# A hybrid mLSTM / GLA / S5 encoder on one core: GpSimd's masks and first exponents earlier, weight splits between the scans, a table stored tile by tile

## The chip, the core and the metric

The kernel runs on one core of one Trainium2 chip. The metric is the device time of one execution in microseconds (us). The core has five engines that run their own instruction streams and meet at semaphores: TensorE (PE in the rows; its weight loads are PEld), VectorE (DVE), ScalarE (ACT), GpSimd (POOL) and SyncE (SP, which here only issues DMAs). ACTq and SPq are the instruction queues of ACT and SP, where DMAs are issued.

## The reference

The input is 256 positions of 2048 channels in float32, through two layers.

- Layer 0: an RMS norm, one combined projection (`w_in`), which feeds an mLSTM (8 heads) and a gated linear attention, GLA (4 heads of 128 key channels), then an output projection (`w_out`), and a residual.
- Layer 1: an RMS norm, an S5 layer (a diagonal complex state space of 64 states for each of 128 groups of channels), GELU and a gate (`glu`), and a residual.
- Behind each: an RMS norm and a convolutional FFN (`up`, a causal convolution of width 3, SiLU times value, `down`, with 5504 inner channels). A last RMS norm ends it.

What the change touches, cut from the reference:

```python
mqk = silu(causal_dwconv(concat([mq, mk]), m_conv_w, m_conv_b))     # width 4
lf = log_sigmoid(f_pre); b = cumsum(lf)                             # mLSTM: sums and a running maximum
log_a = log_sigmoid(glr @ g_w_gate + g_b_gate) / G_TAU              # GLA's forget gate
Bc = cumsum(log_a)
A = einsum("bhtd,bhsd,bhtsd->bhts", qc, kc, exp(Bc_t - Bc_s))       # only for s <= t
lam_bar = exp(lam * dt); pow_t = exp(lam * dt * steps)              # S5: powers of complex numbers
```

## The kernel before, in words

Everything is kept transposed, channels on the 128 partitions and the 256 positions along the row. Each product is done in float32 to more than the precision of one fp32r product. A **block** of weights (128x1024, 512 KB) is loaded by SP into `raw`; ACT writes its rounded part to `hi` (`act_split`, L298), DVE the rest to `lo` (`dve_split`, L305), and PE multiplies both with the two parts `xh`, `xl` of the activations (`pe_tile`). The three rings have four slots; SP refills a slot of `raw` when DVE has split it (`lo_done`), ACT refills one of `hi` when PE has used it (`block_used`). One output tile of 128 channels takes two blocks and goes to one of two banks of PSUM, `acc[q % 2]`. ACT copies one half of the bank (`low_half`), DVE adds the other (`joined`) and counts the tile as read (`tile_read`).

The order on each engine is that of the code in its block function; nothing reorders it. Each waits on semaphores in that order. The stages in order of time:

1. The first norm (to about 27 us). POOL makes constants, then waits for DVE's step sizes of S5 (`s5_dt_new`).
2. Tiles of the gates, of the GLA's q and k (8 tiles) and of the mLSTM's q and k (8 tiles, with a convolution of width 4 on DVE: `conv_tile`, and a SiLU: `silu`). Between the two sets stand DVE's scans: the GLA's running sums `decay` (four, L1184), which `lf_new` announces to POOL, and the mLSTM's rows (L1187 to L1191), announced by `rows_new`. DVE splits two blocks ahead of the tile that it then reads.
3. The values, 32 blocks in 8 steps of 4 (`value_blocks`, L1618 to L1620), and between them the GLA's levels. For level m POOL writes differences of `decay` to `xk` (L667 and L668, `gla_x`), ACT takes the exponential (L857), DVE multiplies by q and k (`gla_scale`, L1243 and L1244), and PE multiplies (`gla_level`, L1641 and L1647). In each step DVE does two splits, then `gla_scale`, then two more splits. From level 1 on, DVE reads a mask made by POOL (`masks_ready`).
4. The output gates with the mLSTM's heads, `w_out`, and the FFN of layer 0. While `w_out` runs, POOL builds the table of S5's turns (`rot_c`, `rot_s`, each 128 x 64 x 64). It lies where the later tiles of the FFN's activations will be written, so it has to be in DRAM (`s5_rot`) before tile `ROT_FREE` = 19 of `up`.
5. `down`, S5, `glu` and the second FFN.

POOL's own stream in stages 2 and 3, before: 8 halvings of an exponential by complex products (L591 to L611), S5's powers (L617 to L635), the seven masks (L637 to L644), the sum of `ident`'s blocks (L650), `skip` (L653), and only then the differences for the GLA.

The loop over `up` is `up_pair(i)`, two tiles a pass: ACT does two splits, `high`, `low_half`, two splits, a tanh and `low_half`; DVE two splits, the product, a convolution, two splits, `low` and a convolution.

Of the kernel before, what the change touches and what calls it, by code (L numbers as in the profile page):

```python
# [13 lines left out]
P = 128  # L14
D = 2048
L = 256
KT = D // P
# [3 lines left out]
M_HEADS, M_DV, M_DK = 8, 128, 64  # L21
# [4 lines left out]
S5_P, S5_N = 16, 64  # L26
# [12 lines left out]
ROT_FREE = 19  # L39
# [56 lines left out]
def hybrid_encoder(nc, t, out):  # L96
# [6 lines left out]
    with ctx:  # L103
# [456 lines left out]
        def _(g):  # L560
# [8 lines left out]
            for j in range(T5):  # L569
                G.memset(steps[:, j, :, :, j], 1.0)  # L570

# [37 lines left out]
            for _ in range(HALVINGS):  # L609
                G.tensor_scalar(zv(14), cur[0], 2.0, None, ADD)  # L610
                chain(G.tensor_scalar(zv(15), cur[1], 1.0, None, MUL))  # L611
                cmul(nxt, cur, (zv(14), zv(15)), ztmp)
                cur, nxt = nxt, cur
            ztmp = (z(12), z(13))
# [22 lines left out]
            chain(G.memset(masks[:, :, :], 0.0))  # L637
            n = P // 2
            for m in range(7):
                v = masks[:, m, :].rearrange("p (j w) -> p j w", w=2 * n)  # L640
                chain(G.memset(v[:, :, n:], 1.0))
                chain(G.affine_select(out=v, in_=v, compare_op=ALU.is_ge, fill=0.0, base=0,
                                      pattern=[[-2 * n, P // (2 * n)], [0, 2 * n]], channel_multiplier=1))
                ins = G.affine_select(out=v, in_=v, compare_op=ALU.is_ge, fill=0.0, base=n - 1,  # L644
                                      pattern=[[2 * n, P // (2 * n)], [0, 2 * n]], channel_multiplier=-1)
                chain(ins) if m < 6 else ins.then_inc(masks_ready, 1)
                n //= 2
            chain(G.memset(rtmp[:, 0, 0:S5_P], 0.0))
            for x in range(P // S5_P):
                chain(G.tensor_tensor(rtmp[:, 0, 0:S5_P], rtmp[:, 0, 0:S5_P],  # L650
                                      ident[:, S5_P * x:S5_P * (x + 1)], ADD))
# [6 lines left out]
            g.wait_ge(lf_new, 1)  # L658
            n = P
            for m in range(8):  # L660
                s = m % 2
                if m >= 2:
                    g.wait_ge(gla_mm, m - 1)
                v = xk[:, s, :, :].rearrange("p h (j a w) -> p (h j) a w", a=2, w=n)
                b = decay[:, :, :].rearrange("p h (j a w) -> p (h j) a w", a=2, w=n)
                mid = b[:, :, 0, n - 1:n].broadcast_to([P, G_HEADS * L // (2 * n), n])
                G.tensor_tensor(v[:, :, 0, :], mid, b[:, :, 0, :], SUB)  # L667
                G.tensor_tensor(v[:, :, 1, :], b[:, :, 1, :], mid, SUB).then_inc(gla_x, 1)  # L668
                n //= 2
# [135 lines left out]
        def _(a):  # L805
# [120 lines left out]
            def ffn(b_up, b_dn, q_up, n, layer):  # L926
# [18 lines left out]
                if layer == 0:  # L945
                    with a.Fori(1, 4) as i:
                        up_pair(i, False)
                    a.wait_ge(rot_whole, 1)
# [166 lines left out]
        def _(v):  # L1115
# [63 lines left out]
            V.memset(neg_m, 0.0)  # L1179
            v.wait_ge(ln_done, 1)  # L1180
            V.scalar_tensor_tensor(rows[:, 3, :], rows[:, 1, :], 0.0, rows[:, 2, :], MIN, SUB)
            chain(V.scalar_tensor_tensor(xk[:, 0, :, :], xk[:, 1, :, :], 0.0, xk[:, 0, :, :], MIN, SUB))
            for x in range(G_HEADS):
                ins = V.tensor_tensor_scan(decay[:, x, :], ones_l[:, :], xk[:, 0, x, :], 0.0, MUL, ADD)  # L1184
            ins.then_inc(lf_new, 1)

            chain(V.tensor_tensor_scan(rows[:, 2, :], ones_l[0:M_HEADS, :], rows[:, 3, :], 0.0, MUL, ADD))  # L1187
            chain(V.tensor_tensor(rows[:, 3, :], rows[:, 0, :], rows[:, 2, :], SUB))
            chain(V.tensor_tensor_scan(rows[:, 5, :], rows[:, 3, :], rows[:, 3, :], 0.0, MAX, MAX))
            V.tensor_scalar(neg_m[0:M_HEADS], rows[:, 5, :], -1.0, None, MUL)  # L1190
            V.tensor_tensor(rows[:, 4, :], rows[:, 2, :], rows[:, 5, :], ADD).then_inc(rows_new, 1)  # L1191

# [21 lines left out]
            def conv_tile(i, m):  # L1214
                dve_split(v, B_IN + 20, 4, i, range(2 * m, 2 * m + 2))
# [5 lines left out]
            conv_tile(0, 0)  # L1221
            conv_tile(0, 1)
# [796 lines left out]
```

## Time and profile before

| | |
|---|---|
| median of 3 runs | 2178.53 us (2175.89 to 2179.95) |
| the profiled execution's own time | 2178.51 us |
| its span in the trace | 2176.8 us |
| PE busy | 2062.1 us, 95% |
| DVE busy | 1600.1 us, 74% |
| ACT busy | 983.6 us, 45% |
| POOL busy | 600.0 us, 28% |
| mean granted clock of TensorE | 0.977 |
| DMA | 398.78 MB, mean 183 GB/s |

The busy share is a mean over the whole span. An engine that is busy 95% of the time still has stretches in which it waits, and a wait in the timeline is shown in brackets behind the instruction that ended it, with what released it. A POOL that is idle for most of the span can still be the last to finish what another engine needs.

### The profile page before, as it was taken

The page shows a single profiled execution, that of the slowest core. Times are in us where ns is not written, and L with a number is a line of the kernel's source. Part 1 is how long each engine was busy: PE and PEld are TensorE (multiplying, and loading weights), DVE is VectorE, ACT ScalarE, POOL GpSimd, SP SyncE. Part 2 cuts the span into 40 slices and gives each one's busy share as a digit, 9 for nine tenths or more (in the row PEclk, how much of TensorE's full clock was granted, in tenths as well). Part 3 has the DMA queues.
Part 4 walks back from the last instruction along what each step waited for, and adds up shares of the span by engine and source line. Part 5 has one row for each costly group of instructions (what it writes and reads, how often), then busy time and mean ns, then how long its engine had stood idle before and what let it go on. Part 6 is the DMA issues. An engine that isn't in the chain of part 4 may idle for free.

```text
span 2176.8 us, 39816 instructions
## 1 busy us (share of the span) xinstructions
PE 2062.1 (95%) x13014; PEld 1790.2 (82%) x13014; DVE 1600.1 (74%) x2333; ACT 983.6 (45%) x1391; POOL 600.0 (28%) x686
## 2 busy tenths in 40 slices
PE   5979999998999999999999977989999999999997
PEld 4757877887888888888888876878888888888886
DVE  7766554777788888888777675778888888875655
ACT  5434344444444444444555513454444444444442
POOL 6991100590000000007888564510000000001221
PEclk9999999998999999999999988999999999999999
DMA  4535533453755555556778884545555555556664
GB/s 167 172 116 168 160 129 124 142 186 121 247 191 193 191 185 185 190 190 197 236 231 235 252 258 135 191 139 186 187 192 192 187 187 187 191 183 195 188 182 140
DMA packets 146680, 398.78 MB, mean 183 GB/s; under 512 B 22704, under 2 KB 47920, under 8 KB 146624
## 3 DMA queue, kind: packets, MB, share of 16 engines
q1 hardware_dynamic: 126176, 379.17, 55.3%
q10 hardware_dynamic: 20448, 18.88, 2.7%
q8 instruction: 33, 0.54, 0.1%
q14 instruction: 23, 0.19, 0.0%
HBM read 377.02 MB, written 18.87 MB: 182 GB/s over the span
## 4 chain that ended last, share of the span: by engine, by line
PE 44%; DVE 26%; issue 14%; POOL 7%; DVEq 3%; ACT 2%; DMA 2%; ACTq 1%; SPq 0%; POOLq 0%
PE bank L325 21%; PE bank L324 11%; DVE lo L305 9%; DVE cgv L1201 4%; DVE cgv L1198 3%; DVE sumt L339 3%; DVE th L1394 2%; ACT lowt L334 1%; DVE aa L1398 1%; DVE cgv L1393 1%; PE bank L1618 1%; PE bank L1620 1%; PE bank L1619 1%; DVEq L1201 1%; PE bank L321 1%
## 5 line engine op out<-in xcount | busy, mean ns | idle before, releaser
L325 PE MATMUL bank<-xx,hi 128*128 128x512 f32 x3420 | 1199.7, 393 | 0.0
L305 DVE TENSOR_TENSOR lo<-raw,hi 128x1024 fp32r<-128x1024 f32 x698 | 881.4, 1294 | 106.4 <-ACT hi L298 104.9
L324 PE MATMUL bank<-xx,lo 128*128 128x256 f32 x3420 | 957.4, 280 | 0.0
L298 ACT ACTIVATE hi<-raw 128x1024 fp32r<-128x1024 f32 x698 | 710.5, 1053 | 324.6 <-PE bank L325 254.9
L325 PEld LDWEIGHTS bank<-xx,hi 128*128 128x128 f32 x3420 | 642.3, 188 | 133.2
L324 PEld LDWEIGHTS bank<-xx,lo 128*128 128x128 f32 x3420 | 644.7, 189 | 10.9 <-issue 0.4
L325 PE MATMUL bank<-aa,hi 128*128 128x512 f32 x1344 | 467.7, 392 | 0.0
L324 PE MATMUL bank<-aa,lo 128*128 128x256 f32 x1344 | 376.1, 280 | 4.7 <-DVE lo L305 4.7
L325 PEld LDWEIGHTS bank<-aa,hi 128*128 128x128 f32 x1344 | 252.4, 188 | 54.4
L324 PEld LDWEIGHTS bank<-aa,lo 128*128 128x128 f32 x1344 | 252.4, 188 | 7.4 <-DVE lo L305 6.0
L1201 DVE SCALAR_TENSOR_TENSOR cgv<-sumt,par,cgv 128x255 f32<-128x255 f32 x368 | 179.5, 488 | 54.4 <-DVE cgv L1201 26.1
L339 DVE TENSOR_TENSOR sumt<-bank,lowt 128x256 f32<-128x256 f32 x212 | 89.5, 422 | 128.6 <-ACT lowt L334 128.0
L933 ACT ACTIVATE aa<-th 128x256 f32 (+1 forms) x86 | 35.9, 418 | 322.8 <-DVE th L1394 322.8
L334 ACT ACTIVATE lowt<-bank 128x256 f32<-128x256 f32 x212 | 80.0, 377 | 214.2 <-PE bank L325 206.4
L345 POOL TENSOR_TENSOR ssq<-h 128x256 f32<-128x256 f32 x2 | 3.0, 1490 | 531.8 <-DVE h L1373 509.8
L733 POOL MEMSET k_win<- 128x256 f32 x1 | 0.3, 314 | 493.9 <-PE bank L325 493.9
L321 PE MATMUL bank<-xx,hi 128*128 128x512 f32 x228 | 93.2, 409 | 15.7 <-DVE lo L305 15.7
L1198 DVE TENSOR_SCALAR cgv<-sumt,par 128x256 f32<-128x256 f32 x180 | 74.8, 416 | 40.7 <-DVE sumt L339 40.4
L1372 DVE TENSOR_TENSOR h<-bank,h 128x256 f32 (+1 forms) x48 | 20.4, 424 | 104.6 <-PE bank L325 103.0
L348 POOL TENSOR_TENSOR sqt<-h 128x256 f32<-128x256 f32 x28 | 40.4, 1443 | 201.2 <-DVE h L1373 166.0
L1618 PE MATMUL bank<-hi,xx 128*128 128x512 f32 x128 | 53.1, 415 | 15.7 <-DVE lo L305 15.7
L759 POOL TENSOR_TENSOR sumt<-bbar,pow_in 128x256 f32<-128x256 f32 x64 | 63.6, 1013 | 2.5
(333 smaller groups left out, 1968.2 us busy)
## 6 DMA issues: line engine op xcount, KB each, us to landing
raw<-in_up SPq DMA_DIRECT2D x344, 512.0 KB, 3.8
raw<-in_down SPq DMA_DIRECT2D x160, 448.0 KB, 4.1
raw<-in_w_in SPq DMA_DIRECT2D x98, 512.0 KB, 4.0
raw<-in_w_out SPq DMA_DIRECT2D x32, 512.0 KB, 3.4
raw<-in_down SPq DMA_DIRECT2D x32, 512.0 KB, 3.6
raw<-in_glu SPq DMA_DIRECT2D x32, 512.0 KB, 3.8
s_c<-cp ACTq DMA_DIRECT2D x16, 256.0 KB, 5.0
s_p<-ut ACTq DMA_DIRECT2D x32, 128.0 KB, 5.2
```

The lines of the kernel that those rows point to most:

```text
L298: A.activation(hi[:, s, :], raw[:, s, :], ACT.Copy).then_inc(hi_done, 1)
L305: V.tensor_tensor(lo[:, s, :], raw[:, s, :], hi[:, s, :].bitcast(f32), SUB).then_inc(lo_done, 1)
L321: TE.matmul(bank[:, :], hi[:, s, w], x2[:, k, :, :], start=True, stop=False)
L324: TE.matmul(bank[:, L:], lo[:, s, w], x2[:, k, 0, :], start=False, stop=False)
L325: last = TE.matmul(bank[:, :], hi[:, s, w], x2[:, k, :, :], start=False, stop=k == total - 1)
L334: A.activation(lowt[:, q % 2, :], acc[q % 2][:, L:], ACT.Copy, **kw).then_inc(low_done, 1)
L339: return V.tensor_tensor(sumt[:, q % 2, :], acc[q % 2][:, 0:L], lowt[:, q % 2, :], ADD)
L759: ins = G.tensor_tensor(pq_pt[:, d], bbar[:, s, :, d, :].unsqueeze(3).broadcast_to([P, 4, S5_P, T5]), pow_in[:, pairs, :, (part + d) % 2]. ...
L1198: chain(V.tensor_scalar(o[:, :], x, par[:, bass.ds(base + taps - 1, 1)], par[:, bass.ds(base + taps, 1)], MUL, ADD))
L1201: ins = V.scalar_tensor_tensor(o[:, d:L], x[:, 0:L - d], par[:, bass.ds(base + taps - 1 - d, 1)], o[:, d:L], MUL, ADD)
L1394: V.scalar_tensor_tensor(th[:, 1, :], cg[:, :], 0.5, cv[:, :], MUL, MUL).then_inc(a_new, 1)
L1618: TE.matmul(banks[half][:, :], xh[:, k, r], hi[:, s, w], start=k == 0, stop=False)
```

## The change

Four edits.

- **POOL.** The masks and the sum of `ident`'s blocks go to the front of POOL's stream, ahead of its wait for the step sizes. The differences for the GLA become a function, `gla_exponents(m)`. Those of levels 0 and 1 are done behind the halvings and ahead of S5's powers; the others stay where they were.
- **DVE.** The splits of the blocks for the first two convolution tiles (`B_IN + 20` and its three successors) were two ahead of each `conv_tile`, both behind all scans. Now two stand ahead of the scans of `decay`, one behind these, and one behind the first `conv_tile`. The rows of the mLSTM go behind that.
- **PE.** In a loop `pe_tile` also waits for `tile_read` where it had none (the tiles with q = 1 plus a multiple of two).
- **ACT.** The table of turns was stored with two DMAs of 2048 KB behind the fourth pass of `up`. Now each of 16 passes issues two DMAs of 128 KB, those of one tile.

```diff
-            if q >= 2:
+            if q >= 2 or not isinstance(q_i, int):
                 p.wait_ge(tile_read, q - 1 + q_i)
...
                 cmul(nxt, cur, (zv(14), zv(15)), ztmp)
                 cur, nxt = nxt, cur
+            def gla_exponents(m):
+
+                s, n = m % 2, P >> m
+                if m >= 2:
+                    g.wait_ge(gla_mm, m - 1)
...
+            g.wait_ge(lf_new, 1)
+            gla_exponents(0)
+            gla_exponents(1)
...
-            g.wait_ge(lf_new, 1)
-            n = P
-            for m in range(8):
...
+            for m in range(2, 8):
+                gla_exponents(m)
...
                 if layer == 0:
-                    with a.Fori(1, 4) as i:
-                        up_pair(i, False)
                     a.wait_ge(rot_whole, 1)
-                    for part, x in enumerate((rot_c, rot_s)):
-                        a.dma_start(s5_rot[:, :, part, :].rearrange("k p n -> p k n"),
-                                    x[:, :, :].rearrange("p (k m) c -> p k (m c)", m=4)).then_inc(rot_out, 16)
-                    with a.Fori(4, ROT_FREE) as i:
+                    with a.Fori(1, KT + 1) as i:
                         up_pair(i, False)
-                    a.wait_ge(rot_out, 32)
+                        for part, x in enumerate((rot_c, rot_s)):
+                            a.dma_start(s5_rot[bass.ds(i - 1, 1), :, part, :].squeeze(0),
+                                        x[:, bass.ds(4 * i - 4, 4), :].rearrange("p m c -> p (m c)")
+                                        ).then_inc(rot_out, 16)
+                    with a.Fori(KT + 1, ROT_FREE) as i:
+                        up_pair(i, False)
+                    a.wait_ge(rot_out, 32 * KT)
```

On DVE, around the scans between the GLA's tiles and the mLSTM's (`decay` is written by the four scans, `sumt` by `joined`, `cgv` by the convolution, `mqk` by `silu`), the kernel before has:

```order
L1179 MEMSET sqt 12x256
L1181 SCALAR_TENSOR_TENSOR ut<-ut 8x256
L1182 SCALAR_TENSOR_TENSOR xk<-xk 128x1024
L1184 SCALAR_TENSOR_TENSOR decay<-ones,xk 128x256 x4
L1187 SCALAR_TENSOR_TENSOR ut<-ones,ut 8x256
L1188 TENSOR_TENSOR ut<-ut 8x256
L1189 SCALAR_TENSOR_TENSOR ut<-ut 8x256
L1190 TENSOR_SCALAR sqt<-ut 8x256
L1191 TENSOR_TENSOR ut<-ut 8x256
L305 TENSOR_TENSOR lo<-raw,hi 128x1024 x2
L339 TENSOR_TENSOR sumt<-bank,lowt 128x256
```

and the changed kernel, in the same place:

```order
L305 TENSOR_TENSOR lo<-raw,hi 128x1024 x2
L1215 MEMSET sqt 12x256
L1217 SCALAR_TENSOR_TENSOR ut<-ut 8x256
L1218 SCALAR_TENSOR_TENSOR xk<-xk 128x1024
L1220 SCALAR_TENSOR_TENSOR decay<-ones,xk 128x256 x4
L305 TENSOR_TENSOR lo<-raw,hi 128x1024
L339 TENSOR_TENSOR sumt<-bank,lowt 128x256
L1190 TENSOR_SCALAR cgv<-sumt,par 128x256
L1193 SCALAR_TENSOR_TENSOR cgv<-sumt,par,cgv 128x255
L1193 SCALAR_TENSOR_TENSOR cgv<-sumt,par,cgv 128x254
L1193 SCALAR_TENSOR_TENSOR cgv<-sumt,par,cgv 128x253
L305 TENSOR_TENSOR lo<-raw,hi 128x1024
```

Two splits have gone ahead of the scans, and one each to both sides of the first convolution; the five rows on `ut` and `sqt` follow the last row shown.

On POOL, at the end of the halvings and of S5's powers (`powers` and `r_step` belong to S5, `xk` and `decay` to the GLA), before:

```order
L634 TENSOR_TENSOR r_step<-nt 128x64
L635 TENSOR_SCALAR powers<-powers 128x320
L637 MEMSET masks 128x896
L641 MEMSET masks 128x64
L642 AFFINE_SELECT masks<-masks 128x128
```

and now, at the end of the halvings:

```order
L611 TENSOR_TENSOR nt<-nt 128x128
L612 TENSOR_TENSOR nt<-nt 128x128
L637 TENSOR_TENSOR xk<-decay 128x4x128
L638 TENSOR_TENSOR xk<-decay 128x4x128
L637 TENSOR_TENSOR xk<-decay 128x8x64
L638 TENSOR_TENSOR xk<-decay 128x8x64
L647 MEMSET powers 128x64
```

The four writes of `xk` stand ahead of `powers`, where before `powers` and the masks stood ahead of them.

## Rows read from the trace of the kernel before

**Rows 1.** The timeline of PE, where it waited (start us, duration us; [wait, releaser]).

```profile
91.89 0.80 PE L321 MATMUL bank<-xx,hi 128*128 128x512 f32 x1 [4.67 <-DVE lo L305]
...
145.59 0.50 PE L1618 MATMUL bank<-hi,xx 128*128 128x512 f32 x1 [2.98 <-DVE lo L305]
...
165.44 0.80 PE L1618 MATMUL bank<-hi,xx 128*128 128x512 f32 x1 [12.42 <-DVE lo L305]
179.00 1.05 PE L1641 MATMUL bank<-xk 128*128 128x128 f32 x8
```

**Rows 2.** The timelines of DVE and ACT where the values begin.

```profile
162.21 1.44 DVE L1243 TENSOR_TENSOR xk<-xk,gqk 128x512 f32<-128x512 f32 x1 [15.04 <-ACT xk L857]
...
161.12 1.06 ACT L857 ACTIVATE xk<-xk 128x1024 f32<-128x1024 f32 x1 [16.65 <-POOL xk L668]
```

**Rows 3.** The timeline of POOL from the halvings' end to the first differences.

```profile
118.84 0.64 POOL L597 TENSOR_TENSOR nt<-nt 128x128 f32<-128x128 f32 x1
...
146.80 0.84 POOL L637 MEMSET masks<- 128x896 f32 x1
...
154.33 0.71 POOL L642 TENSOR_SCALAR_AFFINE_SELECT masks<-masks 128x128 f32<-128x128 f32 x1
...
159.04 1.04 POOL L667 TENSOR_TENSOR xk<-decay 128x512 f32<-128x512 f32 x1
...
162.04 1.06 POOL L668 TENSOR_TENSOR xk<-decay 128x512 f32<-128x512 f32 x1
```

**Rows 4.** Windows: length, busy time (instructions) by engine, PE's granted clock, DMA.

```profile
165.40:170.40 5.00, 4.96 (x12) 3.89 (x13) 4.60 (x5) 1.51 (x2) 0.00 (x0) 0.50 0.70 213
```

**Rows 5.** The timeline of DVE around the scans.

```profile
84.69 3.25 DVE L1184 TENSOR_TENSOR_SCAN decay<-ones,xk 128x256 f32<-128x256 f32 x4
...
90.63 2.34 DVE L305 TENSOR_TENSOR lo<-raw,hi 128x1024 fp32r<-128x1024 f32 x2
...
99.80 0.42 DVE L339 TENSOR_TENSOR sumt<-bank,lowt 128x256 f32<-128x256 f32 x1 [0.92 <-ACT lowt L334]
```

**Rows 6.** Timelines where the table is stored: ACT's queue, DVE, PE.

```profile
549.81 4.79 ACTq L950 DMA_DIRECT2D s_rot<-rot_s  x1
...
555.96 2.36 DVE L305 TENSOR_TENSOR lo<-raw,hi 128x1024 fp32r<-128x1024 f32 x2 [4.08 <-ACT hi L298]
...
557.24 0.51 PE L321 MATMUL bank<-xx,hi 128*128 128x512 f32 x1 [2.55 <-DVE lo L305]
...
563.54 0.50 PE L321 MATMUL bank<-xx,hi 128*128 128x512 f32 x1 [0.48 <-DVE lo L305]
```

**Rows 7.** An earlier pass of `up`, at the same place: ACT and DVE.

```profile
538.02 0.39 ACT L334 ACTIVATE lowt<-bank 128x256 f32<-128x256 f32 x1 [1.63 <-PE bank L325]
538.42 2.01 ACT L298 ACTIVATE hi<-raw 128x1024 fp32r<-128x1024 f32 x2
...
540.67 2.36 DVE L305 TENSOR_TENSOR lo<-raw,hi 128x1024 fp32r<-128x1024 f32 x2
```

**Rows 8.** DMAs issued by ACT in `down`: one line (durations ns), then the timeline.

```profile
L1024 ACTq DMA_DIRECT2D s_p<-ut x32: 622/626/741, 1019.4 to 1253.9; - x32
...
1037.58 2.01 ACT L298 ACTIVATE hi<-raw 128x1024 fp32r<-128x1024 f32 x2 [2.22 <-issue]
```

**Rows 9.** The first norm: timelines of PE, ACT, POOL; a window (DVE is third).

```profile
13.51 0.98 PE L1569 MATMUL bank<-ones,ssq 128*128 128x1 f32 x4 [13.51 <-DVE ssq L1136]
...
16.17 0.26 ACT L370 ACTIVATE root_t<-bank,par 128x2 f32<-128x2 f32 x1
...
19.30 0.15 POOL L575 MEMSET nt<- 128x64 f32 x1 [16.32 <-DVE nt L1146]
...
8.30:13.40 5.10, 0.00 (x0) 0.00 (x0) 4.79 (x5) 2.99 (x3) 0.00 (x0) 1.00 1.02 401
```

**Rows 10.** POOL and DVE at the same time, with the inputs of both in SBUF.

```profile
36.37 2.69 POOL L593 TENSOR_TENSOR nt<-nt 128x128 f32<-128x128 f32 x1
...
36.39 2.34 DVE L305 TENSOR_TENSOR lo<-raw,hi 128x1024 fp32r<-128x1024 f32 x2
```

More of the change, by code:

```diff
@@ L570, in _ @@
                 G.memset(steps[:, j, :, :, j], 1.0)
+            chain(G.memset(masks[:, :, :], 0.0))
+            n = P // 2
+            for m in range(7):
+                v = masks[:, m, :].rearrange("p (j w) -> p j w", w=2 * n)
+                chain(G.memset(v[:, :, n:], 1.0))
+                chain(G.affine_select(out=v, in_=v, compare_op=ALU.is_ge, fill=0.0, base=0,
+                                      pattern=[[-2 * n, P // (2 * n)], [0, 2 * n]], channel_multiplier=1))
+                ins = G.affine_select(out=v, in_=v, compare_op=ALU.is_ge, fill=0.0, base=n - 1,
+                                      pattern=[[2 * n, P // (2 * n)], [0, 2 * n]], channel_multiplier=-1)
+                chain(ins) if m < 6 else ins.then_inc(masks_ready, 1)
+                n //= 2
+            chain(G.memset(rtmp[:, 0, 0:S5_P], 0.0))
+            for x in range(P // S5_P):
+                chain(G.tensor_tensor(rtmp[:, 0, 0:S5_P], rtmp[:, 0, 0:S5_P],
+                                      ident[:, S5_P * x:S5_P * (x + 1)], ADD))
             TWO_PI = (6.28125, 1.9350051879882812e-3, 3.0199157663e-7)
@@ L613, in _ @@
                 cur, nxt = nxt, cur
+            def gla_exponents(m):
+                s, n = m % 2, P >> m
+                if m >= 2:
+                    g.wait_ge(gla_mm, m - 1)
+                v = xk[:, s, :, :].rearrange("p h (j a w) -> p (h j) a w", a=2, w=n)
+                b = decay[:, :, :].rearrange("p h (j a w) -> p (h j) a w", a=2, w=n)
+                mid = b[:, :, 0, n - 1:n].broadcast_to([P, G_HEADS * L // (2 * n), n])
+                G.tensor_tensor(v[:, :, 0, :], mid, b[:, :, 0, :], SUB)
+                G.tensor_tensor(v[:, :, 1, :], b[:, :, 1, :], mid, SUB).then_inc(gla_x, 1)
+            g.wait_ge(lf_new, 1)
+            gla_exponents(0)
+            gla_exponents(1)
             ztmp = (z(12), z(13))
@@ L635, in _ @@
             chain(G.tensor_scalar(powers[:, :, :, 2], powers[:, :, :, 1], -1.0, None, MUL))
[L637 to L651, printed above, removed]
             g.wait_ge(params_in, 16)
@@ L1177, in _ @@
                     gqk_tile(i, m)
[L1179 to L1191, printed above, removed]
             def conv(q, low, used, o, base, taps):
@@ L1212, in silu, with conv_tile @@
                                              cgv[:, 0:1, :], ADD, MUL))
-            def conv_tile(i, m):
-                dve_split(v, B_IN + 20, 4, i, range(2 * m, 2 * m + 2))
+            def conv_tile(i, m, split=True):
+                if split:
+                    dve_split(v, B_IN + 20, 4, i, range(2 * m, 2 * m + 2))
                 if m == 1:
@@ L1220, in conv_tile @@
                 conv(9 + m, 9 + m + 2 * i, 10 + m + 2 * i, cg, COLS["mconv"] + 5 * (2 * i + m), 4)
-            conv_tile(0, 0)
-            conv_tile(0, 1)
+            dve_split(v, B_IN + 20, 4, 0, range(2))
+            V.memset(neg_m, 0.0)
+            v.wait_ge(ln_done, 1)
+            V.scalar_tensor_tensor(rows[:, 3, :], rows[:, 1, :], 0.0, rows[:, 2, :], MIN, SUB)
+            chain(V.scalar_tensor_tensor(xk[:, 0, :, :], xk[:, 1, :, :], 0.0, xk[:, 0, :, :], MIN, SUB))
+            for x in range(G_HEADS):
+                ins = V.tensor_tensor_scan(decay[:, x, :], ones_l[:, :], xk[:, 0, x, :], 0.0, MUL, ADD)
+            ins.then_inc(lf_new, 1)
+            dve_split(v, B_IN + 20, 4, 0, range(2, 3))
+            conv_tile(0, 0, False)
+            dve_split(v, B_IN + 20, 4, 0, range(3, 4))
+            chain(V.tensor_tensor_scan(rows[:, 2, :], ones_l[0:M_HEADS, :], rows[:, 3, :], 0.0, MUL, ADD))
+            chain(V.tensor_tensor(rows[:, 3, :], rows[:, 0, :], rows[:, 2, :], SUB))
+            chain(V.tensor_tensor_scan(rows[:, 5, :], rows[:, 3, :], rows[:, 3, :], 0.0, MAX, MAX))
+            V.tensor_scalar(neg_m[0:M_HEADS], rows[:, 5, :], -1.0, None, MUL)
+            V.tensor_tensor(rows[:, 4, :], rows[:, 2, :], rows[:, 5, :], ADD).then_inc(rows_new, 1)
+            conv_tile(0, 1, False)
             with chain.loop(1, 4, 2 * 4) as i:
```

11 lines of the change are left out of this document (1 added, 10 removed).

## The prediction, as it went on record

> **What bounds the kernel now.** I read the page first: PE is busy 95% of the span, so the time is PE's work plus the few stretches in which it stands still, and a change that leaves PE's work alone can gain only from these. The view of who waited for whom, limited to PE, then names them, and the timelines of PE, ACT, DVE and POOL around each show what ended it.
>
> The longest is at 165.44 us, where PE has stood for 12.42 us for a split of DVE [rows 1]. Follow it back. DVE's split stood behind its first product for the GLA, at 162.21, for which it had waited 15.04 us [rows 2]. That waited for ACT's exponential at 161.12, and ACT had waited 16.65 us for POOL's differences [rows 2]. POOL was not waiting at all: it ended the halvings at 119.48, was in S5's powers until 146.8, in the masks, the sum of `ident`'s blocks and `skip` until 159.04, and then wrote the differences of levels 0 and 1, until 163.10 [rows 3]. Nothing of what it did between is needed by the first level. So the wait is one of order on POOL. Behind it PE also ran at the lower of its two levels: 5.00 us at a granted clock of 0.50, that is at 1.2 in place of 2.4 GHz [rows 4].
>
> The second place is `up`, where ACT's queue spent 4.79 us on issuing the second half of the table. DVE lost 4.08 us on it and PE 2.55 us, and 0.48 us a tile later [rows 6]. The third is at 91.89, where PE stood 4.67 us because all scans stood ahead of the splits [rows 1, 5]. That one must not be counted as a gain without more: see below.
>
> **The POOL edit.** The masks and the sum took at most 146.80 to 159.04, 12.2 us [rows 3]. At the front they run from about 3.0 us (POOL had stood still for 16.32 us before 19.30) to about 15.2 us, ahead of the wait for the step sizes, which ended at 19.30 [rows 9]. They cost POOL nothing. The halvings then end at 119.5 as before. The differences of levels 0 and 1 took 159.04 to 163.10, 4.1 us [rows 3], and now run from 119.5 to 123.6. S5's powers end at 146.8 + 4.1 = 150.9. The next differences wait for PE's first level, which will come later than that, so POOL is not late again.
>
> Next I ask what is late in its place. ACT was free for the exponential at 161.12 - 16.65 = 144.47, DVE for the product at 162.21 - 15.04 = 147.17 [rows 2]. The exponential takes 1.06 us, so it ends at 145.5, ahead of DVE. From DVE's product to PE's first matmul on the block behind it were 165.44 - 162.21 = 3.23 us [rows 1, 2], so this block is ready at 147.17 + 3.23 = 150.4. PE had used up its older blocks at 165.44 - 12.42 = 153.02. PE is later by 2.6 us, so its wait goes whole: **12.42 us**. Nothing takes its place; the 2.98 us before 145.59 [rows 1] are DVE's split behind the convolutions, which the edit leaves. The low clock goes with the long standstill: 5.00 us at half speed did the work of 2.5, a gain of **2.5 us**. The clock's fall at 145.59, behind the shorter wait, stays.
>
> **The DVE edit.** From the scans to the values DVE is the bound: PE waits for a split of DVE at nearly each tile there, and DVE's timeline has hardly a gap. The edit takes no work from DVE. What it can gain is DVE's own idle time: 0.92 us at 99.80 [rows 5], where DVE waited for a tile that PE had started late, at 91.89. Now PE gets its two blocks ahead of the scans and starts this tile at 91.89 - 4.67 = 87.2. PE's wait of 4.67 us does not vanish, though, it moves. A tile takes PE about 5.8 us (557.24 to 563.54 less the wait of 0.48 [rows 6]), so two tiles on, at 98.8, it wants two blocks more. DVE has the same work as before up to the read at 99.80, so it comes to this at 98.9; a convolution and a split later, at about 103, it has the block. PE will stand there for about 4 us. That costs nothing as long as DVE is the bound, since DVE reads the tile that PE then starts only behind two pairs of splits (2.34 us a pair [rows 5]) and another convolution, some 8 us later. Against the 0.92 us stands that the four differences of POOL now fall beside DVE's work, at 119.5 to 123.6. The bounds are a gain of 0.9 us, if they hold DVE up not at all, and a loss of 4.1 - 0.9 = 3.2 us, if DVE stands for their whole length. POOL was busy beside DVE there before, too, so I take a gain of **0.7 us**, near the first bound.
>
> PE's new wait for `tile_read` bites at one place only, the tile that starts at about 93 us: it needs the first convolution's tile to be read. DVE does that behind the scans, the two splits ahead of them and one more: 84.69 + 3.25 + 2.34 + 1.17 = 91.5 us, and PE comes at 87.2 + 5.8 = 93. It costs nothing that shows.
>
> **The first norm.** The masks now run beside DVE's sums of squares. PE's first matmul waits for these, and ends at 13.51 + 0.98 = 14.49, but ACT's root comes at 16.17 [rows 9], behind ACT's own work. So the sums have 1.7 us in hand. From 8.3 to 13.4 us DVE does five sums in 4.79 us [rows 9], each of two inputs in SBUF. At 36.37 an instruction of POOL lasted 2.69 us, to the end of the two splits of DVE that ran from 36.39 [rows 10]: each of the two engines can hold the other. The longest instruction of the masks took 0.71 us [rows 3]. If each of the five sums stood behind one such, they would end 3.6 us later, of which 1.9 us show; if none did, nothing. I take zero, since the sum of the masks' selects is small in this stretch.
>
> The Trainium skill's page "SBUF — State Buffer", section "Who interferes with whom", says that a VectorE instruction with two SBUF inputs and a GpSimd instruction that reads SBUF exclude each other for their whole length, and that whichever issues second blocks. The row at 36.37 agrees. By that rule the upper end of 1.9 us could come about, and it is kept as a rival.
>
> **The ACT edit.** The 4.79 us of issuing go, and with them the 2.55 + 0.48 = **3.03 us** of PE. In their place 16 passes issue two DMAs of 128 KB each. DMAs of 128 KB issued by ACT took 0.62 to 0.74 us each, and three DMAs with their registers held ACT for 2.22 us [rows 8]. So two hold it for 1.3 to 1.7 us. What do they delay? ACT's two splits, which came right behind `low_half`, at 538.42; the first ended at 539.4, and DVE wanted it at 540.67 [rows 7]: 1.2 us in hand. Behind that DVE is ahead of PE by 4.08 - 3.03 = 1.05 us [rows 6], so PE sees nothing until ACT is late by 2.3 us a pass. The issue also begins while `low_half` still runs. So it is hidden, at a price of 0; bounds are 0 and, should two DMAs hold ACT as long as twice the 2.22 us, 16 x (4.44 - 2.3) = 34 us. The value is near the first bound, because two DMAs are less than the three that took 2.22. The table has landed long before the wait at pass 19, two passes of two tiles behind the last store.
>
> **The sum.** 12.42 + 2.5 + 0.7 + 3.03 = 18.65 us. The profiled execution took 2178.51 us (its span 2176.8, and 1.7 around it), and the median of the runs is 2178.53, so no correction is needed: 2178.5 - 18.6 = **2159.9 us**. Behind each of the places all engines wait for each other in the same order as before, and no transfer or chain runs on its own clock over a stage, so a shift is carried to the end.
>
> **Rivals.**
> - *The stores cost passes of `up`.* For it: they are on ACT, whose splits DVE needs, and DVE and PE keep pace almost exactly there. Against it: the 2.3 us in hand. If two DMAs hold ACT for 2.6 us, each pass loses 0.3 us, 16 x 0.3 = 5 us: 2165. Chance 0.10.
> - *Slower than before.* The same mechanism, in its strong form: the queue holds the issuing engine whenever earlier descriptors have not drained, as the second DMA's 4.79 us may be read. At 0.5 + 4.79 = 5.3 us a pass, PE would lose 16 x (5.3 - 2.3) = 48 us: 2208. It decides from 2.3 + 18.6 / 16 = 3.5 us a pass. Against it: the 4.79 us came behind 2 MB, not 128 KB, and three DMAs of `down` took 2.22. Chance 0.03.
> - *The lock in the first norm* costs its 1.9 us: 2162. Chance 0.07.
> - *POOL holds DVE in the convolutions*: the differences and the powers, which now also run beside DVE's first products, cost 3 us: 2163.5. Chance 0.08.
> - *The wait for the first level is not gone but only taken over*, by something between POOL and ACT that I do not see, and half of 14.9 us is lost: 2167. Chance 0.03.
> - *More than forecast*: PE's short standstill at 145.59 and its low clock shrink, too, because DVE comes out of the convolutions earlier than by 0.7: 2156. Chance 0.07.
>
> **How the numbers follow.** The forecast has 0.62, with 2158 to 2162 as its own range. Two tenths outside: 2157 at the low end takes in all but the last rival, and 2165.5 at the high end takes in the norm, POOL and the usual form of the stores. Slower by over 0.2% (4.4 us, about what a measurement of this kernel can tell from no change) is the second rival, 0.03; within it 0.01; faster 0.96.
>
> **What would show it.** Right: ACT's first exponential at about 144 us with no wait for POOL; no wait of PE between 150 and 164; the first level (before at 179.00) at about 163.4; a granted clock of 1.00 from 153 on; a wait of PE of 4 to 5 us at about 103 and none at 92; no wait of PE in `up` behind the table; S5's powers ending at about 151. Wrong: a wait of PE at each of the first 16 passes of `up` (the stores); ACT's root later than 16.2 us (the norm); DVE's first product for the GLA later than 147.2 (DVE held by POOL); a wait for POOL's differences of level 2.

## The result and the profile after

| | before | after |
|---|---|---|
| median | 2177.35 us (2175.89 to 2179.95, 4 runs) | 2162.21 us (2160.33 to 2163.56, 4 runs) |
| ratio, with its 95% interval | | 0.9929 (0.9911 to 0.9946) |
| the profiled execution's own time, span | 2178.51, 2176.8 us | 2161.42, 2159.7 us |
| mean granted clock | 0.977 | 0.980 |

The change gains 15.1 us by the medians; 18.65 had been forecast against a before of 2178.5. The time, 2162.2, lies 2.3 us above the forecast of 2159.9, inside the range and 0.2 us outside the likeliest case's own.

The timeline of PE after, where it waited up to the values, and the first level:

```profile
97.54 0.39 PE L324 MATMUL bank<-xx,lo 128*128 128x256 f32 x1 [0.45 <-DVE lo L305]
104.95 0.80 PE L321 MATMUL bank<-xx,hi 128*128 128x512 f32 x1 [4.36 <-DVE lo L305]
126.47 0.50 PE L321 MATMUL bank<-xx,hi 128*128 128x512 f32 x1 [2.21 <-DVE lo L305]
...
166.15 1.05 PE L1651 MATMUL bank<-xk 128*128 128x128 f32 x8
```

The 12.42 us at 165.44 [rows 1] are gone and nothing took their place. The wait of 4.67 us at 91.89 [rows 1] has become one of 4.36 at 104.95: moved, not removed. The 2.21 us at 126.47 stand behind the convolution that runs beside POOL's four differences (before, the wait at this tile was 0.72 us). The first level is at 166.15 in place of 179.00; about 163.4 had been forecast. The window that held the low clock [rows 4] lay at 165.4 us; over 145 to 170 us the rows of both kernels are (PE is the second number, PE's granted clock stands behind POOL's):

```profile
145.00:170.00 25.00, 11.99 (x35) 9.17 (x36) 9.95 (x11) 5.79 (x6) 15.86 (x37) 0.67 0.25 79
```

```profile
145.00:170.00 25.00, 22.73 (x95) 18.09 (x95) 17.00 (x17) 12.09 (x13) 15.19 (x16) 0.93 0.52 168
```

The first is before, the second after: PE is busy for 22.7 us in place of 12.0, at a clock of 0.93 in place of 0.67. ACT and DVE after, at the first exponential and product, which answer to [rows 2]:

```profile
146.47 1.04 ACT L862 ACTIVATE xk<-xk 128x1024 f32<-128x1024 f32 x1
...
148.92 0.69 DVE L1253 TENSOR_TENSOR xk<-xk,gqk 128x512 f32<-128x512 f32 x1
```

Neither has a bracket: the waits of 16.65 and 15.04 us are gone. Both come later than foreseen, by 2.0 and 1.7 us. POOL after, against [rows 3]:

```profile
120.49 1.04 POOL L637 TENSOR_TENSOR xk<-decay 128x512 f32<-128x512 f32 x1
...
123.73 1.24 POOL L638 TENSOR_TENSOR xk<-decay 128x512 f32<-128x512 f32 x1
...
155.03 1.34 POOL L665 TENSOR_SCALAR powers<-powers 128x320 f32<-128x320 f32 x1
...
167.35 1.04 POOL L637 TENSOR_TENSOR xk<-decay 128x512 f32<-128x512 f32 x1 [9.34 <-PE bank L1651]
```

The differences are written 38 us earlier. S5's powers end at 156.4, not at 151, and then POOL waits for PE 9.34 us, so it is never the last at level 2.

The table's store after, against [rows 6] (ACT's queue, then ACT):

```profile
515.95 0.42 ACTq L955 DMA_DIRECT2D s_rot<-rot_c  x1
516.57 0.36 ACTq L955 DMA_DIRECT2D s_rot<-rot_s  x1
517.36 2.01 ACT L298 ACTIVATE hi<-raw 128x1024 fp32r<-128x1024 f32 x2 [1.23 <-issue]
```

Each of the 16 passes holds ACT for 1.1 to 1.2 us, and PE has no wait above 0.2 us between 505 and 570 us.

**Where the time went, along the program.** PE runs the same 13014 matmuls in the same order in all kernels of this study, so the start of the same matmul can be compared. The table gives its shift against before (median over six neighbours; minus is earlier), each in one profiled execution.

| matmul that starts, before, at | 30 | 140 | 180 | 250 | 528 | 575 | 1200 | end |
|---|---|---|---|---|---|---|---|---|
| after | +1.3 | +2.9 | -12.9 | -12.9 | -11.1 | -14.7 | -15.2 | -17.1 |
| masks back behind the powers | +0.1 | +0.8 | -15.6 | -15.6 | -13.7 | -17.3 | -17.7 | -25.0 |
| without DVE's and PE's edit | +1.5 | +3.5 | -12.1 | -12.1 | -10.2 | -13.8 | -14.3 | -11.3 |
| before + differences ahead | -0.2 | +1.8 | -15.3 | -15.4 | -12.9 | -12.2 | -12.7 | -15.3 |
| before + masks at the front | +1.5 | +2.0 | -10.1 | -10.1 | -10.0 | -10.1 | -9.8 | -13.8 |
| before + table by tiles | -0.2 | +0.1 | +0.5 | +0.5 | +2.2 | -1.3 | -1.8 | -5.7 |
| before + DVE's and PE's edit | +0.1 | -1.0 | +0.8 | +0.8 | +2.5 | +3.4 | +2.9 | -2.2 |
| powers late | -0.2 | +1.5 | -16.2 | -16.2 | -16.2 | -19.7 | -20.2 | -22.1 |
| five halvings late | -0.4 | -3.3 | -19.1 | -19.1 | -19.7 | -23.2 | -23.7 | -23.9 |
| the same kernel again | -0.2 | -2.3 | -18.5 | -18.5 | -18.9 | -22.5 | -23.0 | -30.4 |
| six halvings late, masks earlier | -0.1 | -2.8 | -18.9 | -18.9 | -19.3 | -22.8 | -23.3 | -27.4 |

Read after from left to right: 1.3 us lost in the first norm, 1.6 more in the convolutions, 15.8 gained at the values, 1.8 lost again by 528 us (most of it in the first tiles of the FFN), 3.6 gained at the table, 0.5 in `down`, and 1.9 in S5, where the change does nothing. The last column needs care: two executions of one kernel (rows nine and ten of the table) stand 0.7 us apart at 1200 and 6.5 apart at the end. The windows from 1200 to 1500 us of the two (columns as above):

```profile
1200.00:1500.00 300.00, 261.65 (x2700) 231.83 (x2699) 217.08 (x337) 121.90 (x191) 109.88 (x90) 0.93 0.62 191
```

```profile
1200.00:1500.00 300.00, 266.57 (x2741) 236.11 (x2740) 222.94 (x347) 124.95 (x195) 110.52 (x91) 0.94 0.64 197
```

The second was granted a clock of 0.94 where the first had 0.93, and got further in the same 300 us. A clock higher by 0.01 over 300 us makes, as an estimate, 3 us; the rest of what they differ by is not traced here. So up to 1200 us the traces are compared below, and the end is left to the medians. The same two rows also say how far two executions of one kernel differ ahead of that: 1.0 us at 140, 0.6 at 180 and 0.7 at 1200. A difference between two kernels that is no larger is not shown by one trace of each.

### The profile page after: what moved, and what is told of

It is laid out like the page before. It is cut to its first block, busy times and chain, and to the rows that moved or that the text cites. A ratio compares the mean times of both kernels' runs of the same rounds, so it can differ in the third digit from the quotient of the medians.

```text
span 2159.7 us, 39918 instructions
## 1 busy us (share of the span) xinstructions
PE 2057.3 (95%) x13014; PEld 1787.2 (83%) x13014; DVE 1602.3 (74%) x2333; ACT 983.2 (46%) x1391; POOL 609.9 (28%) x686
## 4 chain that ended last, share of the span: by engine, by line
PE 46%; DVE 30%; issue 14%; DVEq 3%; ACT 2%; POOL 1%; DMA 1%; ACTq 1%; POOLq 0%
PE bank L325 22%; PE bank L324 11%; DVE lo L305 11%; DVE cgv L1193 5%; DVE cgv L1190 3%; DVE sumt L339 3%; DVE th L1404 2%; ACT lowt L334 1%; DVE cgv L1403 1%; PE bank L1628 1%; PE bank L1630 1%; PE bank L1629 1%; DVE aa L1408 1%; PE bank L321 1%; DVEq L1193 1%
## 5 line engine op out<-in xcount | busy, mean ns | idle before, releaser
L324 PE MATMUL bank<-xx,lo 128*128 128x256 f32 x3420 | 959.2, 280 | 0.4 <-DVE lo L305 0.4
L1193 DVE SCALAR_TENSOR_TENSOR cgv<-sumt,par,cgv 128x255 f32<-128x255 f32 x368 | 180.6, 491 | 54.4 <-DVE cgv L1193 26.1
L322 PE MATMUL bank<-xx,lo 128*128 128x256 f32 x228 | 64.3, 282 | 0.0
```

Source lines behind the costliest of these rows:

```text
L322: last = TE.matmul(bank[:, L:], lo[:, s, w], x2[:, k, 0, :], start=False, stop=False)
L324: TE.matmul(bank[:, L:], lo[:, s, w], x2[:, k, 0, :], start=False, stop=False)
L1193: ins = V.scalar_tensor_tensor(o[:, d:L], x[:, 0:L - d], par[:, bass.ds(base + taps - 1 - d, 1)], o[:, d:L], MUL, ADD)
```

## The experiments

**Masks back.** From the changed kernel, masks and sum go back behind the powers; all else stays.

```diff
-            chain(G.memset(masks[:, :, :], 0.0))
...
             chain(G.tensor_scalar(powers[:, :, :, 2], powers[:, :, :, 1], -1.0, None, MUL))
+            chain(G.memset(masks[:, :, :], 0.0))
...
             for m in range(2, 8):
                 gla_exponents(m)
```

> The changed kernel with the masks and the sum of ident's blocks back behind S5's powers. Theory (the masks at the front hold up DVE's sums of squares): ACT's root at 16.2 us in place of 17.6, 1.4 us less: 2160.8 us. POOL then ends the masks at about 167 us, and the differences of level 2 come 1 to 3 us later than in the changed kernel, which DVE's splits behind them have in hand. Rival (the first norm is late for another reason): root at 17.6 us and 2162.2 us.

Measured: 2159.48 us (2148.92 to 2161.77, 6 runs), ratio to before 0.9909 (0.9887 to 0.9930). The interval reaches that of the changed kernel, so the times alone don't decide between them. The trace does. ACT's root is where it was before [rows 9]:

```profile
16.14 0.26 ACT L370 ACTIVATE root_t<-bank,par 128x2 f32<-128x2 f32 x1
```

and the kernel is ahead of the changed one by 1.2 us at 30, by 2.7 at 180 (there the clock was granted whole, 1.00 in place of 0.93 over 145 to 170 us) and by 2.5 at 1200. So the masks at the front cost, and their move gains nothing once the differences stand ahead of them.

**Masks alone.** The reverse: before with the masks at the front and nothing else.

> The kernel before with the masks and the sum at the front of POOL, and nothing else. Theory: the root is 1.4 us late, POOL's differences come 11.5 us earlier less these 1.4, so PE's wait falls from 12.4 us to about 1, and with it some of the low clock: 10 to 12 us less, 2166 us. Rival (the first norm is late for another reason than the masks): root at 16.2 us. A plain sum of this run's gain and that of the differences' alone must not give the whole, since either takes away the same wait.

Measured: 2165.89 us (2164.74 to 2168.27, 4 runs), ratio 0.9946 (0.9926 to 0.9965). ACT, POOL and PE:

```profile
17.58 0.26 ACT L370 ACTIVATE root_t<-bank,par 128x2 f32<-128x2 f32 x1
...
149.64 1.04 POOL L667 TENSOR_TENSOR xk<-decay 128x512 f32<-128x512 f32 x1
...
156.05 0.58 PE L1618 MATMUL bank<-hi,xx 128*128 128x512 f32 x1 [2.59 <-DVE lo L305]
```

The root is late by 1.4 us, as in the changed kernel to 0.01: the masks are the cause. The differences come 9.4 us earlier than before, and PE still waits 2.59 us of the 12.42.

**Differences alone.** Before, with levels 0 and 1 ahead of the powers; masks, splits and table as before.

```diff
+            g.wait_ge(lf_new, 1)
+            gla_exponents(0)
+            gla_exponents(1)
...
+            for m in range(2, 8):
+                gla_exponents(m)
```

> The kernel before with one edit: the differences of levels 0 and 1 ahead of S5's powers; the masks stay behind these. Theory (POOL's order is the cause, and nearly all of it is these four instructions): PE's wait of 12.4 us and the low clock behind it go, less 1.2 us that the differences cost DVE: 13.7 us less, 2163.6 us. Rival (the masks at the front are what gives the time): the wait stays at 12.4 us and the time at 2177.

Measured: 2164.06 us (2161.95 to 2166.28, 4 runs), ratio 0.9935 (0.9915 to 0.9956). This one edit, of the order of four instructions, carries most of the gain: 12.7 of 15.2 us at 1200. The rival that the masks at the front are what gives the time is out. PE at the first blocks of the values and at the first level:

```profile
146.75 0.50 PE L1623 MATMUL bank<-hi,xx 128*128 128x512 f32 x1 [2.29 <-DVE lo L305]
...
163.66 1.05 PE L1646 MATMUL bank<-xk 128*128 128x128 f32 x8
```

Between the two PE has no wait above 0.25 us: the 12.42 us are gone by this edit alone, and the clock granted over 145 to 170 us is 1.00. What it costs shows in DVE. First before, then this kernel, at the same convolution:

```profile
119.99 0.47 DVE L1198 TENSOR_SCALAR cgv<-sumt,par 128x256 f32<-128x256 f32 x1 [0.27 <-DVE sumt L339]
120.62 0.48 DVE L1201 SCALAR_TENSOR_TENSOR cgv<-sumt,par,cgv 128x255 f32<-128x255 f32 x1 [0.16 <-DVE cgv L1198]
121.25 1.18 DVE L1201 SCALAR_TENSOR_TENSOR cgv<-sumt,par,cgv 128x254 f32<-128x254 f32 x2 [0.15 <-DVE cgv L1201]
```

```profile
119.50 1.18 DVE L1203 TENSOR_SCALAR cgv<-sumt,par 128x256 f32<-128x256 f32 x1 [0.27 <-DVE sumt L339]
120.84 1.03 DVE L1206 SCALAR_TENSOR_TENSOR cgv<-sumt,par,cgv 128x255 f32<-128x255 f32 x1 [0.16 <-DVE cgv L1203]
122.02 2.22 DVE L1206 SCALAR_TENSOR_TENSOR cgv<-sumt,par,cgv 128x254 f32<-128x254 f32 x2 [0.15 <-DVE cgv L1206]
```

0.47 + 0.48 + 1.18 = 2.13 us became 1.18 + 1.03 + 2.22 = 4.43, beside the four differences of POOL, which ran from 119.49 for 4.5 us. DVE's first split of the values ended 1.2 us later than before (146.70 for 145.54).

**DVE's and PE's edit alone.** Before with the splits between the scans and the wait for `tile_read`.

> The kernel before with DVE's order around the scans and PE's wait changed, and nothing else. Theory (the values start when POOL's differences come): PE's wait at 165 us ends when it did, so no change, 2177.3 us, with the wait of 4.7 us moved from 92 to about 103 us. Rival (it gives PE's wait and the low clock behind it): 6 us less, 2171 us.

Measured: 2177.66 us (2169.93 to 2187.91, 10 runs), ratio 1.0000 (0.9984 to 1.0016). No change. The trace tells why; PE:

```profile
102.76 0.50 PE L321 MATMUL bank<-xx,hi 128*128 128x512 f32 x1 [3.90 <-DVE lo L305]
...
166.07 0.79 PE L1622 MATMUL bank<-hi,xx 128*128 128x512 f32 x1 [14.23 <-DVE lo L305]
```

The wait at 92 moved to 103. DVE's first split of the values ended 1.0 us earlier (144.55 for 145.54). That is no more than two executions of one kernel can differ by. But the wait behind the first product then grew from 12.42 to 14.23, and the matmul that ended it came no earlier than before (166.07 for 165.44): POOL sets that meeting, and who arrives earlier waits longer.

**Without DVE's and PE's edit.** The changed kernel with only these two undone.

> The changed kernel with the order of DVE and the wait of PE as before. Theory (DVE is the bound of the convolutions, so PE's wait of 4.7 us only moved): at most 0.9 us more than the changed kernel, 2162.6 us; PE waits 4.7 us near 93 us and not at 105. Rival (the edit is worth PE's wait and the low clock behind it): 6 us more, 2168 us.

Measured: 2165.05 us (2161.62 to 2167.43, 6 runs), ratio 0.9937 (0.9922 to 0.9952). This kernel is behind the changed one by 0.6 us at 140, by 0.8 at 180 and by 0.9 at 1200 in the table above. With POOL out of the way the edit may be worth that much, but two executions of one kernel differ by as much there (0.6 to 1.0 us), and the medians stand 2.8 apart with intervals that overlap: that it gains anything is not shown. The median lies between the 2162.6 expected and the rival's 2168; the rival's 6 us don't show in the trace, and 2168 lies just beyond the interval.

**The table by tiles, alone.**

> The kernel before with the table stored tile by tile, and nothing else. Theory: PE's waits of 2.55 and 0.48 us go, 3.0 to 3.4 us less, 2174.2 us. Rival (the first passes of up pay for the 32 DMAs, which would explain 1.7 us that the changed kernel lost at the start of up): 1.7 us less, 2175.7 us, and PE behind by 1.7 us at the second pass also where the granted clock is 1.00.

Measured: 2173.18 us (2169.10 to 2177.81, 10 runs), ratio 0.9977 (0.9963 to 0.9990), a gain of 5.0 by the ratio. In the table, this kernel moves from +2.2 to -1.3 between 528 and 575: 3.5 us. Each of the eight rows with the store by tiles gains 3.5 or 3.6 there; of the three without it two lose 0.7 and 0.9, and one gains 0.1. So the size is firm and does not hang on the other edits. The rival, that the first passes of `up` pay 1.7 us for the DMAs, is out: the same 1.4 to 1.6 us are lost between 510 and 528 in two kernels without these DMAs (the differences alone, DVE's and PE's edit alone), and not lost in four that have them (see the low clock below).

**Powers late.** If the masks cost in the norm and the powers beside the convolutions, both can go where POOL waits for PE. Masks behind the differences of levels 0 and 1, S5's powers behind level 7.

```diff
             gla_exponents(0)
             gla_exponents(1)
+            chain(G.memset(masks[:, :, :], 0.0))
...
+            for m in range(2, 8):
+                gla_exponents(m)
...
-            for m in range(2, 8):
-                gla_exponents(m)
```

> The changed kernel, but on POOL the masks stand behind the differences of levels 0 and 1, and S5's powers behind those of level 7. Theory (POOL and DVE hold each other up): ACT's root comes at 16.2 us again and not at 17.6, since nothing runs beside DVE's sums of squares, which is worth 1.4 us; from about 137 us on POOL is idle beside the last convolutions, each of which then takes DVE some 0.5 us less, worth 1 to 2 us more. About 2159 us against 2162.2 for the changed kernel and 2177.3 for the one before. Rival (the 1.4 us and the late DVE are chance or come from the new order on DVE): the root stays at 17.6 us, DVE's first split of the values at 146.5, and the time at 2162.

Measured: 2159.09 us (2156.37 to 2162.91, 6 runs), ratio 0.9917 (0.9901 to 0.9933). As the theory had it, and 5.0 us ahead of the changed kernel at 1200: 1.5 of them stand at 30 us, 1.8 more come by 180, and 1.8 by 528, where this execution ran at full clock. The last part can't be laid to the edit, and the intervals of the medians overlap.

**Five halvings late.** Of the 8 halvings only three (`EARLY`) stay ahead; five go between the levels 2 to 7, in each of which POOL waits for PE.

```diff
-            for _ in range(HALVINGS):
+            for _ in range(EARLY):
+                halving()
...
             for m in range(2, 8):
                 gla_exponents(m)
+                if m < 7:
+                    halving()
```

> As the kernel with late powers, and five of the eight halvings stand between the differences of levels 2 to 7, so that POOL does only the first two differences and the masks between about 91 us and the values. Theory (POOL and DVE hold each other up, and DVE is the bound of the convolutions): a tile of the convolutions takes DVE about 5.8 us in place of 6.5, so the values start 4 to 6 us earlier, and the time is about 2154 us. Rival (DVE's pace there is its own): 2159 to 2162 us. Rival (POOL becomes late in the heads): slower than 2162, with waits for POOL behind 280 us.

Measured: 2153.04 us (2151.84 to 2154.87, 4 runs), ratio 0.9883 (0.9864 to 0.9902): faster than the changed kernel too, the intervals don't touch. The gain over powers late is made in the convolutions, where DVE is the bound: 4.8 us at 140, of which 3.5 are left at 1200 (3.8 and 2.8 in the second execution of the table). The rival that POOL becomes late in the heads is out: the shift is -19.1 at 250 us and -19.7 at 528. DVE there:

```profile
123.94 0.41 DVE L1194 TENSOR_SCALAR cgv<-sumt,par 128x256 f32<-128x256 f32 x1 [0.27 <-DVE sumt L339]
124.50 1.74 DVE L1197 SCALAR_TENSOR_TENSOR cgv<-sumt,par,cgv 128x255 f32<-128x255 f32 x3
126.16 2.35 DVE L305 TENSOR_TENSOR lo<-raw,hi 128x1024 fp32r<-128x1024 f32 x2
```

A pair of splits takes 2.35 us, where with POOL at the halvings one took 2.88 (before and after alike, at 115.67 and 116.60). The stretch from DVE's splits for the GLA's last tile to the end of its first split of the values, in the changed kernel and in this one (DVE is third, POOL fifth):

```profile
79.08:147.69 68.61, 59.37 (x305) 50.15 (x303) 60.10 (x82) 27.35 (x40) 66.09 (x96) 0.93 0.44 143
```

```profile
77.23:141.35 64.12, 56.88 (x305) 47.75 (x303) 55.59 (x82) 27.43 (x40) 29.51 (x47) 0.97 0.47 153
```

It is 4.5 us shorter with POOL busy for 29.5 us of it in place of 66.1, and DVE is busy with the same 82 instructions for 55.6 us in place of 60.1: the whole gain is in how long DVE's instructions last, none in its idle time. That cost had been there in the kernel before, and neither the change nor the prediction saw it.

**The same again, and POOL cleared further.** Run together: the same kernel, and one with six halvings late and the masks between the early halvings and the wait for the running sums.

> The version with five late halvings once more, to hold its gain over the changed kernel against the spread that the number of low-clock stretches makes between executions of one kernel. Theory that the gain is POOL's absence beside DVE: again 2153 us (2151.5 to 2155), DVE's first split of the values at about 141 us, and what differs from the earlier trace lies behind 1200 us, where S5 begins. Rival, that the earlier runs had a lucky clock: 2157 to 2160 us.

> The version with five late halvings, carried on: only two halvings stand ahead of the first differences, six behind the later ones, and the masks stand between the halvings and the wait for the running sums, so that beside DVE's scans and convolutions POOL does nothing but the differences of levels 0 and 1. Theory that POOL's work costs DVE there in proportion to how long POOL is busy: from DVE's split ahead of the scans to its first split of the values it took 68.60 us in the changed kernel with POOL busy for 68.8, and 64.11 us with five late halvings and POOL busy for 29.8, so 0.115 us for each us of POOL. With POOL busy for about 15 us it takes about 62.5 us, and the time comes to about 2151.5 us. Rival, that only the long products of the halvings hold DVE and masks do not: 64.1 us as before, and 2153 us. A second rival, that the masks now cost DVE's splits between 69 and 81 us what they cost it later: the stretch is shorter, but the first split of the values comes no earlier than at 141.3 us, and the time stays at 2153.

Measured: again 2153.00 us (2148.25 to 2155.32, 6 runs), ratio 0.9883 (0.9863 to 0.9903); cleared further 2154.11 us (2151.19 to 2158.27, 6 runs), ratio 0.9890 (0.9869 to 0.9910). The median of the first repeats to 0.04 us, so its gain is no luck of the clock. The second gains nothing. The halvings ended at 81.4 us, later than I had taken, so the masks and the sum ran until 99.5, beside the scans, and POOL was still busy for 26.1 us of the stretch. (The 68.8 in the expectation is longer than the stretch of 68.6 itself: it adds up durations that overlap. Counted once, POOL was busy for 66.1, and the price is (68.6 - 64.1) / (66.1 - 29.5) = 0.12 us for each of POOL's.) By that the stretch would take 63.7 us, and it took 63.9. But the rivals, 64.1 us and a first split no earlier than at 141.3 (it ended at 141.62), fit as well, and the same kernel again took 64.7. So the run did not decide between them: POOL was not cleared. That the long products alone hold DVE stays possible.

## Why the prediction was right, and where it was not

**The wait for POOL's order, 12.42 us: right.** It went whole, and the experiments with one edit each show that the differences ahead of the powers do it by themselves.

**The low clock behind it, 2.5 us: right.** From 140 to 180 us PE gained 15.8: the 12.42, 0.7 of a shorter wait at the first block (2.98 to 2.27), and 2.7 left for the clock. The clock's fall behind the first, short wait stayed, as forecast (0.51 over 147.7 to 151.1 us, 1.00 from there to 170). Not foreseen was a stretch of low clock at about 503 us that puts PE back by 1.4 us in the first tiles of the FFN. Before and after, over the same piece of work:

```profile
515.40:518.40 3.00, 2.93 (x17) 2.59 (x18) 2.89 (x7) 2.71 (x5) 0.00 (x0) 1.00 0.55 175
```

```profile
502.80:505.80 3.00, 2.93 (x9) 2.54 (x10) 2.89 (x7) 2.71 (x5) 0.00 (x0) 0.50 0.55 178
```

PE is as busy in both, and does 17 matmuls in one and 9 in the other, at half the clock. The step of 1.4 to 1.6 us between 510 and 528 stands in six of the twelve traces; before, masks alone and the four with late powers are without it. In all twelve PE had waited 2.2 us for DVE's split at this tile; in six the clock was then halved and in six it was not. I can't lay it to an edit.

**DVE's idle time, 0.7 us with what POOL holds taken off: the step failed, inside its bounds.** By one trace each the edit itself gives 0.7 to 1.0 us (without it, and it alone), as said, but two executions of one kernel differ by up to 1.0 us there, so this is not shown. The idle time it was to take is gone: DVE reads the second convolution's tile at 100.86 with no wait, where it had waited 0.92 at 99.80 [rows 5]. The four differences cost DVE 1.2 us in the trace of the differences alone (2.3 us at the convolution beside them), where I had put 0.2 with the argument that POOL was busy beside DVE there before, too. It was, but DVE still lost to the differences; the net is a loss of 0.2 to 0.5 us from these runs, and 0.75 in the changed kernel's own trace (its first split of the values ended at 147.69 for 145.54, 1.4 of it from the norm). The bounds reached from a gain of 0.9 to a loss of 3.2.

**PE's wait for `tile_read`, 0: right.** No row of PE names it. **The wait of 4.67 us moves to about 103: right**, 4.36 at 104.95.

**The first norm, taken at 0: this is the step that failed.** The only ground given for zero was that the sum of the masks' selects is small in this stretch, with no number beside it. It cost 1.4 us (ACT's root at 17.57 in place of 16.17 [rows 9]), most of the 1.9 that the rival had as its upper end. The rows of before and after, DVE first:

```profile
2.89 0.20 DVE L1121 TENSOR_SCALAR nt<-nt 128x64 f32<-128x64 f32 x1 [2.89 <-DMA nt<-in_lam]
...
8.38 1.23 DVE L1131 TENSOR_TENSOR vals<-vals 128x1024 f32<-128x1024 f32 x1 [0.66 <-ACT vals L810]
```

```profile
2.87 0.91 DVE L1127 TENSOR_SCALAR nt<-nt 128x64 f32<-128x64 f32 x1 [2.87 <-DMA nt<-in_lam]
...
9.79 1.32 DVE L1137 TENSOR_TENSOR vals<-vals 128x1024 f32<-128x1024 f32 x1
```

```profile
2.88 0.85 POOL L571 MEMSET masks<- 128x896 f32 x1
...
11.76 1.31 POOL L578 TENSOR_SCALAR_AFFINE_SELECT masks<-masks 128x128 f32<-128x128 f32 x1
13.02 0.11 POOL L582 MEMSET rtmp<- 128x16 f32 x1
13.21 4.29 POOL L584 TENSOR_TENSOR rtmp<-rtmp,ident 128x16 f32<-128x16 f32 x8
```

I had asked what the masks do to the five sums of squares. They do little: from the first to the end of the last 4.98 us before and 5.26 after. So the rival had a size near the measured one, but not its path. The loss is ahead of them, in DVE's small operations on S5's step sizes, 2.89 to 7.72 us before and 2.87 to 9.76 after: 2.1 us more, of which 0.7 fall on DVE's wait for ACT (the 0.66 in the bracket). And the 1.7 us that I had put in hand were not there. Before, PE's matmul ended at 14.49 [rows 9], ACT's own split at 14.86, and then ACT loaded a table for the root:

```profile
13.80 1.06 ACT L298 ACTIVATE hi<-raw 128x1024 fp32r<-128x1024 f32 x1 [0.22 <-DMA raw<-in_w_in]
14.87 1.28 ACT L370 ACT_TABLE_LOAD   x1
```

The load of 1.28 us lies behind both, so only 14.86 - 14.49 = 0.37 us were in hand. In the changed kernel the load waits for PE:

```profile
15.20 0.99 PE L1579 MATMUL bank<-ones,ssq 128*128 128x1 f32 x4 [15.20 <-DVE ssq L1142]
...
16.27 1.28 ACT L370 ACT_TABLE_LOAD   x1 [1.73 <-PE bank L1579]
17.57 0.26 ACT L370 ACTIVATE root_t<-bank,par 128x2 f32<-128x2 f32 x1
```

PE's matmul is late by 1.69 us, the root by 1.40. The timeline of ACT between the two would have told that.

The Trainium skill's page "SBUF — State Buffer", section "Who interferes with whom", has VectorE's instructions with two SBUF inputs and GpSimd's reads of SBUF lock each other out. The trace agrees for POOL's side: a select that lasts 0.70 us by itself lasted 1.31 beside a sum, and the eight small additions 4.29 in place of 2.30. The same section says that a DVE instruction with at most one SBUF input does not contend outside the two-port modes, which `tensor_scalar` can enter; here a TENSOR_SCALAR of 128x64 lasted 0.91 us in place of 0.20, beside a memset of POOL that ended with it. Whether it ran in such a mode no run here shows. The prediction's row at 36.37 [rows 10] shows the exclusion, but not who blocks: POOL's instruction started 0.02 us ahead of DVE's splits, and it was the one that lasted until both were done.

**The stores' gain, 3.03 us: right, a little small;** 3.5 us between 528 and 575 in every kernel that has it. **Their price, 0: right.** ACT was held for 1.1 to 1.2 us a pass, below the 1.3 to 1.7 estimated and below the 2.3 in hand.

**S5's powers at 151: wrong by 5.4 us, without effect.** They took 31.5 us (124.9 to 156.4) in place of 27.3, beside other work of DVE than before; that DVE's instructions held them is the likely reason, not one that a run separates. Nor did the masks end at 15.2, as forecast, but at 17.50, and POOL's wait for the step sizes at 20.73 in place of 19.30.

**The sum.** At 1200 us, ahead of S5, 15.2 us are gained where 18.65 were forecast. By the steps of the table, measured less forecast: the norm -1.3; the convolutions -2.3 (a loss of 1.6 for a gain of 0.7); the values +0.9 (15.8 for 14.92); by 528 us -1.8, most of it the low clock at 503; the table +0.6; `down` +0.5. Together -3.4. That the time is off by only 2.3 us has a part of luck: the median before came out at 2177.35, 1.2 us below the 2178.5 that the forecast started from. Two of the prediction's own signs of being wrong came true, ACT's root later than 16.2 us (17.57) and DVE's first product later than 147.2 (148.92). The profiled execution shows 17.1 in the end because S5 took it 1.9 us less than it took the profiled execution of before; the medians (15.1) have no such gain.

## What to carry to other kernels

Look for what the last engine did just ahead of the thing that is waited for: four instructions of GpSimd in another place were worth 13 of 15 us. Work on GpSimd is not free because GpSimd has time: where VectorE sets the pace, GpSimd's work beside it can lengthen both, and it belongs where GpSimd would wait for PE or where PE is the bound (five complex products and their factors, moved there, gave 3 to 6 us more). An edit that brings one engine forward to a meeting which another engine sets gains nothing by itself (2177.66 us for 2177.67).

## What the runs showed of the hardware that was not expected

- POOL beside DVE stretches even DVE's smallest operations: twenty instructions of 0.20 to 0.24 us on S5's step sizes went from 4.8 to 6.9 us in all. A convolution's four steps of 2.1 us took 4.4 beside four differences. Over a stretch bound by DVE, the same 82 instructions kept it busy for 60.1 us with POOL busy for 66.1, and for 55.6 with POOL busy for 29.5.
- Two executions of one kernel differed by 7.2 us in S5 alone (-0.2 and -7.4 from 1200 to the end), with the granted clock between 1200 and 1500 us at 0.93 or 0.94. A gain below that can be seen in traces only ahead of this stage, where the two differ by up to 1.0 us, and in medians only with many runs.
- Two DMAs of 128 KB took 0.42 and 0.36 us to issue, against 4.79 us for one of 2 MB behind another [rows 6].
